# Two gated linear-recurrence blocks behind a transformer: key and query norms through a matrix of ones, the delta rule's preparation one level earlier

## What is computed

```
def _l2norm(x):
    return x * lax.rsqrt(jnp.sum(x * x, axis=-1, keepdims=True) + EPS)

def _gated_delta_rule(q, k, v, beta, g):        # chunks of 64 tokens
    gc = jnp.cumsum(g.reshape(b, h, n, c), axis=-1)
    decay = jnp.exp(jnp.where(incl, gc[..., :, None] - gc[..., None, :], -jnp.inf))
    kb = k * beta[..., None]
    a = jnp.where(strict, jnp.einsum('bhntd,bhnsd->bhnts', kb, k) * decay, 0.0)
    t_inv = lax.linalg.triangular_solve(a + eye, ...)      # (I + A)^-1
    qk = jnp.einsum('bhntd,bhnsd->bhnts', q, k) * decay
    ...

def _mixer(h, w_in, ...):
    p = h @ w_in
    (qkv, z, beta_r, a_r, hq, hf_fwd, hf_bwd, hi, hgate, gate_dn, gate_hg) = _split(p, IN_SIZES)
    qkv = jax.nn.silu(_dwconv(qkv, dn_conv))
    q = _l2norm(_to_heads(q, DN_HEADS)) * (DN_HEAD_DIM ** -0.5)
    k = _l2norm(_to_heads(k, DN_HEADS))
    ...
```

## Time and profile before

| | us |
|---|---|
| median of three runs | 2322.2 (2317.95 to 2328.46) |
| the profiled execution, its own time | 2322.91 |
| its span in the profile | 2320.8 |
| TensorE busy | 2208.2 (95% of the span) |
| VectorE, ScalarE, GpSimd busy | 1556.5, 1053.2, 183.9 |
| `square_sums` to `hg_o`, first mixer layer | 1372.06 to 1488.69 (starts) |

### The profile page before, as it was taken

The page is one execution under the profiler, slowest core; times in us unless marked ns, Lnnn a source line. Parts: engine busy times, 40 slices in busy tenths (PEclk is TensorE's granted clock), DMA queues, the critical chain, the costliest instruction groups (busy, mean ns, idle before and its releaser), DMA issues.

```text
span 2320.8 us, 39379 instructions
## 1 busy us (share of the span) xinstructions
PE 2208.2 (95%) x15834; PEld 2061.6 (89%) x15834; DVE 1556.5 (67%) x2334; ACT 1053.2 (45%) x1488; POOL 183.9 (8%) x157
## 2 busy tenths in 40 slices
PE   7999989999999999999998998999999998999997
PEld 7998869989999998798997998898998998898996
DVE  4557656755575575667557678867677678867676
ACT  4335465533353445554333555434344555434342
POOL 0000000131000000000000006300000006300000
PEclk9999989999999999999999999999999999999999
DMA  7454424475555554344553442214554432214553
GB/s 254 181 183 164 161 73 164 142 206 190 206 198 183 182 187 157 123 150 166 187 191 132 165 144 91 74 55 159 186 181 163 174 135 91 74 55 167 188 181 127
DMA packets 52667, 359.12 MB, mean 155 GB/s; under 512 B 6401, under 2 KB 6785, under 8 KB 11073
## 3 DMA queue, kind: packets, MB, share of 16 engines
q1 hardware_dynamic: 46928, 340.81, 41.4%
q0 software_dynamic: 4336, 13.37, 2.1%
q10 hardware_dynamic: 1280, 3.19, 0.4%
HBM read 356.29 MB, written 1.05 MB: 154 GB/s over the span
## 4 chain that ended last, share of the span: by engine, by line
PE 77%; DVE 12%; ACT 5%; DMA 4%; issue 2%; SPq 0%; DVEq 0%; POOLq 0%; ACTq 0%
PE tile L755 42%; PE acc L791 19%; PE tile L771 6%; DMA ring<-weights 4%; DVE ring_lo L1814 3%; PE tile L1082 3%; PE tile L1280 2%; ACT w_hi L1351 2%; PE tile L927 1%; PE tile L901 1%; PE tile L806 1%; DVE work L2304 1%; DVE work L2302 1%; DVE bn L2199 1%; PE tile L914 1%
## 5 line engine op out<-in xcount | busy, mean ns | idle before, releaser
L1814 DVE TENSOR_TENSOR ring_lo<-ring,w_hi 128x1024 fp32r<-128x1024 f32 x648 | 785.8, 1244 | 608.2 <-ACT w_hi L1351 605.8
L1351 ACT ACTIVATE w_hi<-ring 128x1024 fp32r<-128x1024 f32 x648 | 657.5, 1053 | 938.9 <-DMA ring<-weights 713.8
L755 PE MATMUL tile<-xT_hi,w_hi 128*128 128x256 f32 x3008 | 858.1, 285 | 16.8 <-DVE xT_lo L1805 13.9
L755 PE MATMUL tile<-xT_lo,w_hi 128*128 128x256 f32 x3008 | 853.0, 284 | 0.0
L755 PE MATMUL tile<-xT_hi,ring_lo 128*128 128x256 f32 x3008 | 852.9, 284 | 0.0
L755 PEld LDWEIGHTS tile<-xT_hi,w_hi 128*128 128x128 f32 x3008 | 579.2, 193 | 23.2 <-issue 12.3
L755 PEld LDWEIGHTS tile<-xT_lo,w_hi 128*128 128x128 f32 x3008 | 579.3, 193 | 2.2
L755 PEld LDWEIGHTS tile<-xT_hi,ring_lo 128*128 128x128 f32 x3008 | 579.0, 192 | 0.0
L791 PE MATMUL acc<-w_hi,hidden_hi 128*128 128x512 f32 x528 | 207.9, 394 | 5.5 <-DVE ring_lo L1814 5.5
L791 PE MATMUL acc<-w_hi,hidden_lo 128*128 128x512 f32 x528 | 207.2, 392 | 0.0
L791 PE MATMUL acc<-ring_lo,hidden_hi 128*128 128x512 f32 x528 | 206.6, 391 | 0.0
(11 more groups left out here) (272 smaller groups left out, 2740.7 us busy)
## 6 DMA issues: line engine op xcount, KB each, us to landing
ring<-weights SPq DMA_DIRECT2D x324, 1024.0 KB, 4.8
work<-ln_g_rows POOLq DMA_DIRECT2D x8, 512.0 KB, 6.1
work<-ln_b_rows POOLq DMA_DIRECT2D x8, 512.0 KB, 6.8
work<-rpb POOLq DMA_DIRECT2D x32, 96.0 KB, 14.3
x<-x_in SPq DMA_DIRECT2D x1, 1024.0 KB, 8.0
work<-mem_in ACTq DMA_DIRECT2D x1, 1024.0 KB, 6.6
out<-x POOLq DMA_DIRECT2D x1, 1024.0 KB, 4.4
work<-hmask_in ACTq DMA_DIRECT2D x1, 840.0 KB, 8.5
```

The costliest lines, as they stand in the source:

```text
L755: j = mm(ps[:, f * S:(f + 1) * S], w[a][:, k, :], x2[b][:, k, :], start=(k == 0 and i == 0), stop=(k == KT - 1 and i == 2))
L1351: A(high_of(u, h), half_of(ring, u, h), ACT.Copy).then_inc(sems["w_hi"], 1)
L1814: V.tensor_tensor(half_of(ring_lo, u, h), half_of(ring, u, h), high_of(u, h).bitcast(F32), ALU.subtract).then_inc(sems["w_lo"], 1)
```

## The change

- `square_sums` becomes four matmuls of 512 columns with the 128 x 128 matrix of ones as weights: each sum comes out spread over all partitions, in four tiles (`l2` has four instead of one).
- ScalarE computes from them, between its SiLUs of `hz` and `z`, the factor by logarithm and exponential: four `Ln` from PSUM into `l2s`, four `Exp` in place, with one table set named for both. The root, the reciprocal and the tiles `l2B` go. VectorE multiplies queries and keys by `l2s` out of SBUF between the low parts of the units that `z` feeds.
- `G` moves from level 3 to 2, `kv_T` from 4 to 3, `QK` from 5 to 4. `near_start` moves from behind `args` of level 3 to between the two halves of gate unit 2.
- The gate unit's halves are placed one by one: level 7 now gets the first half of gate unit 7, level 8 the second. The substitution's rows stand behind halves of gate units 3 to 7 and behind levels 4 to 8.
- GpSimd's list is reordered so that the decays are masked one `qmul` earlier.
- Two constants for the logarithm's bias are written by VectorE once, before the first mixer.

```diff
-PREP.update({0: (("gcB0", 2),), 1: (("gcB1", 2),), 2: (("l2B", 4),),
-             3: (("G", 2),), 4: (("kv_T", 4),), 5: (("QK", 2),)})
-GATE_AT = {k: k for k in range(7)}
-GATE_AT[8] = 7
+PREP.update({0: (("gcB0", 2),), 1: (("gcB1", 2),), 2: (("G", 2),), 3: (("kv_T", 4),), 4: (("QK", 2),)})
+GATE_AT = {k: ((k, 0), (k, 1)) for k in range(7)}
+GATE_AT[7] = ((7, 0),)
+GATE_AT[8] = ((7, 1),)
-NEAR_IN_GATE = {4: ((0, 7), (1, 7)), 5: ((0, 7), (1, 3), (1, 7)), 6: ((0, 7), (1, 3), (1, 7)), 7: ((0, 7),)}
+NEAR_AFTER_HALF = ((3, 0), (3, 1), (4, 0), (4, 1), (5, 0), (5, 1), (6, 0), (6, 1), (7, 0))
...
                 def square_sums():
-                    pe.wait_ge(sems["l2_sq"], 4 * l + 4)
-                    ps = open_tile(T[("l2", l)])
-                    for c in range(16):
-                        i = mm(ps[:, c:c + 1], l2s[:, c // 2, (c % 2) * P:(c % 2 + 1) * P], table("ones")[:, 0:1],
-                               start=True, stop=True)
-                    i.then_inc(sems["tile_ready"], 1)
+                    for j in range(4):
+                        pe.wait_ge(sems["l2_sq"], 4 * l + j + 1)
+                        ps = open_tile(T[("l2", l)] + j)
+                        mm(ps[:, :], table("ones"), pair(l2s, j), start=True, stop=True).then_inc(sems["tile_ready"], 1)
...
+                nc.scalar.preload_act_table_set("natural_log_exp_and_others")
+                for j in range(4):
+                    t = T[("l2", l)] + j
+                    act.wait_ge(*ready(t))
+                    A(pair(l2s, j), bank[t % NB][:, :], ACT.Ln, bias=l2_eps[:, 0:1] if j < 2 else l2_eps[:, 1:2],
+                      scale=float(P) if j < 2 else 1.0).then_inc(tile_taken[t % NB], 1)
+                for j in range(4):
+                    act.wait_ge(*taken(T[("l2", l)] + j))
+                    A(pair(l2s, j), pair(l2s, j), ACT.Exp, scale=-0.5).then_inc(sems["l2_inv"], 1)
...
-                for j in range(2):
-                    feed_one("z", j)
+                feed_one("z", 0)
+                for j in range(4):
+                    dve.wait_ge(sems["l2_inv"], 4 * l + j + 1)
+                    V.tensor_tensor(pair(qkvT, j), pair(qkvT, j), pair(l2s, j), ALU.mult).then_inc(sems["l2_done"], 1)
+                feed_one("z", 1)
...
+                    for g, half in GATE_AT[k]:
+                        if half == 0 and k < LEVELS:
+                            args(l, k + 2)
+                        if half == 1 and k == 2:
+                            near_start()
+                        if (g, half) in NEAR_AFTER_HALF:
                             near_step(next(rows))
+                        feed(U[("gate", l, g)], halves=(half,))
...
-                for k in range(1, 4):
+                for k in range(1, 3):
                     qmul(k)
-                    if k > 1:
-                        decays_of(2 * k - 4)
-                        decays_of(2 * k - 3)
-                qmul(4)
+                    decays_of(2 * k - 2)
+                    decays_of(2 * k - 1)
+                qmul(3)
```

More of the change, by code:

```diff
@@ L624, in build @@
         note = small[:, 13, :]
-        l2n, l2i, ngc = [small[:, i, :] for i in range(14, 17)]
+        l2_eps, ngc = small[:, 14, 0:2], small[:, 16, :]
         ba32 = small[:, 0:2, :].rearrange("p a b -> p (a b)")
@@ L743, in await_x, with features @@
                 pe.wait_ge(sems["x_lo"], 4 * plan.sets[name] + q + 1)
-            def features(u, t, x_set=None, more=0, x2=x2, between=None):
-                for f in range(2):
+            def features(u, t, x_set=None, more=0, x2=x2, halves=(0, 1)):
+                for f in halves:
                     w = open_half(u, f, KT, more)
-                    if f == 0:
-                        ps = open_tile(t, more)
+                    ps = open_tile(t, more) if f == 0 else bank[t % NB]
                     for k in range(KT):
@@ L1196, in mixer2 @@
                     prepare(k)
-                    if k in GATE_AT:
-                        g = GATE_AT[k]
-                        features(U[("gate", l, g)], T[("gate", l, g)],
-                                 between=lambda f, j: (f, j) in NEAR_IN_GATE.get(g, ()) and near_row(next(rows)))
+                    for g, half in GATE_AT[k]:
+                        features(U[("gate", l, g)], T[("gate", l, g)], halves=(half,))
+                        if (g, half) in NEAR_AFTER_HALF:
+                            near_row(next(rows))
                 for c in range(2):
@@ L1740, in mixer2 @@
                     prepare(k)
-                    if k in GATE_AT:
-                        feed(U[("gate", l, GATE_AT[k])])
-                        take(T[("gate", l, GATE_AT[k])], pair(gates, GATE_AT[k]))
+                    for g, half in GATE_AT[k]:
+                        split_half(U[("gate", l, g)] + 2, half)
+                        if half == 1:
+                            take(T[("gate", l, g)], pair(gates, g))
                 for g in range(4):
@@ L2419, in prepare @@
                     if k == 2:
-                        for j in range(4):
-                            t = T[("l2B", l)] + j
-                            dve.wait_ge(*ready(t))
-                            V.tensor_tensor(pair(qkvT, j), pair(qkvT, j), bank[t % NB][:, :], ALU.mult).then_inc(tile_taken[t % NB], 1)
-                        for j in range(4):
-                            dve.wait_ge(*taken(T[("l2B", l)] + j))
-                        dve.sem_inc(sems["l2_done"], 1)
-                    if k == 3:
                         for tt in range(TT):
@@ L2470, in mixer2 @@
                     prepare(k)
-                    at = NEAR_IN_GATE.get(GATE_AT.get(k), ())
-                    for f, j in at:
-                        if f == 0:
-                            near_step(next(rows))
-                    if k < LEVELS:
-                        args(l, k + 2)
-                    if k == 3:
-                        near_start()
-                    if k in GATE_AT:
-                        for f, j in at:
-                            if f == 1 and j < KT - 1:
-                                near_step(next(rows))
-                        feed(U[("gate", l, GATE_AT[k])], halves=(0,))
-                        for f, j in at:
-                            if f == 1 and j == KT - 1:
-                                near_step(next(rows))
+                    for g, half in GATE_AT[k]:
+                        if half == 0 and k < LEVELS:
+                            args(l, k + 2)
+                        if half == 1 and k == 2:
+                            near_start()
+                        if (g, half) in NEAR_AFTER_HALF:
+                            near_step(next(rows))
+                        feed(U[("gate", l, g)], halves=(half,))
                         if k == LEVELS + 1:
```

63 lines of the change are left out of this document (24 added, 39 removed).

## The result

The median of five executions of the changed kernel is 2310.66 us (2303.78 to 2314.39) against 2323.21 (2317.95 to 2328.46) before. The ratio is 0.9943, 95% interval 0.9922 to 0.9963: 12.6 us or 0.57% faster. Forecast were 2312.5 us and a range of 2305 to 2321. Repeated beside other kernels the changed one took 2311.23 us, ratio 0.9943 again (0.9923 to 0.9963).

What follows compares the result with a forecast made beforehand. TensorE, busy for 95% of the span, was taken as the bound, with its waits and lowered clock. Terms of -4.4 us (first layer), -6.2 (second) and 0.3 lost gave -10.3 us, so 2312.5 us, range 2305 to 2321.

Steps and rivals of the forecast that it cites:

- Norms and clock: From sums to level 0: full-array sums keep the clock up over `z`, saving 2.4 us (first layer), 4.2 (second).
- Spreading the norms: Dropping `l2B` saves 3.6 us a layer; its gather wait moves to gate unit 2 as 2.6 us, 0.4 lost.
- Start of the substitution: `near_start` a level sooner: 5.9 us of waiting moves to the third `kv_T` tile, clock falls as before; no gain.
- Last level: Half a gate unit between levels 7 and 8 covers `qmul(8)`; the wait goes, 2.7 us saved a layer.
- The rows: Substitution rows at new places wait 7.2 us for VectorE's steps; 2.9 us lost a layer, bounds 0 and 5.1.
- Behind the walk: At the third `W0` tile TensorE waits, as `x_first` stands behind the last low part; 1.0 us lost a layer.
- Rival 1: Clock stays up behind the `kv_T` wait: 2.2 us more saved a layer, 2308 us; chance 0.25.
- Rival 2: Clock still falls at the norms, taking back some 7.2 us: 2319.7 us; chance 0.22 together with Rival 3.
- Rival 3: The gather wait at gate unit 2 swallows the norms' saving, 6.4 us: 2319 us; chance 0.22 together with Rival 2.
- Rival 4: GpSimd's six operations between levels 5 and 8 each hit a substitution step: slower, 2337 us; chance 0.08.

Runs made afterwards that it cites:

- the best kernel: Changed kernel with the multiplies by beta moved to ScalarE and unread filler matmuls at `kv_T`, `W0` and in the recursion: 2302.54 us, ratio 0.9909.

## Why the forecast held, step by step

The 2312.5 us itself has a small slip in it: -10.3 us from the profiled execution is 2312.6, and an execution 0.7 us above the median puts the median at 2311.9. Of the chances, 0.37 went to a gain of more than 0.5%, and the 0.57% measured fell there, not into the 0.55 for less.

**Norms and clock: right.** -2.6 and -4.1 against -2.4 and -4.2. 1.6 us of the second layer's share hung on which profile of before it was read from. The added wait was 0.3 us, not 0.8. The load and the logarithm took what was forecast (load from 1365.25, next pass at 1366.55, so 1.30 and no drain), but the SiLU ahead of them began 1.2 us behind the sums' start instead of 1.7. Over all profiles with the new norms this wait is 0.3 to 0.7 us. That thin matmuls bring the clock down was argued in the prediction and is shown by the kernel that put them back.

**Spreading the norms: right, with a wait missed.** Gate unit 2 waits 2.26 us on the gather (forecast 2.6), but gate unit 1 waits 0.66 as well, which I had not: 0.7 us lost instead of 0.4. The second profile of before has a wait of 0.54 us at gate unit 1 in its first layer, so part of this is not the change's.

**Start of the substitution: right on the wait, the clock's part a little too dear.** The wait went to the third `kv_T` tile, 5.0 and 6.1 us against a forecast of 5.9, and the clock falls behind it as before. But only eight of the sixteen transposes stand behind it now; the other eight run at full clock ahead of it. Without the wait the sixteen take 2.7 us, where they took 3.5 to 3.6 in the first profile of before; in the second layer half of this 0.9 us goes again in the gate unit behind them, which takes more of the fall. The first layer's wait is shorter because TensorE arrived later: a half-clock stretch in gate unit 2 cost 1.5 us, 1.1 of which the wait gave back.

**Last level: right in the changed kernel, too small as a price.** The 2.7 us wait is gone. Undoing the split cost 4.2 us up to `hg_o`, since the wait is 3.4 us in the new order and a clock fall follows it.

**The rows: the term that was mis-sized.** Three waits of 1.10, 1.64 and 0.80 us, 3.5 in all against 2.1: 1.4 us lost, where I had 2.9. The prediction asked for 5 to 7 us on L2448, and this was wrong. Three of its five places were right, rows 5 and 8 and the hit of `qmul(8)` on row 12's step, each 0.4 to 0.6 us shorter than I had them; the 1.9 us for `qmul(7)` did not come. Row 8's step had ended 0.2 us before `qmul(7)` began (1453.75, 1453.93). So level 0 to `hg_o` gave 4.7 to 5.0 us instead of 3.0, the rows' 1.5 us being the larger part of the difference and the transposes a smaller one, and hg_o came 7.5 and 8.9 us sooner, beyond the 7 that I had named as the limit (in the repeated changed kernel's first layer, at 110.7, it is 5.9). The bound of 0 to 5.1 held it.

**Behind the walk: right.** 1.2 us of wait, 1.3 in all, against 1.0.

**What no term had: the late fall.** It took back 3.2 us of the first layer, so the sum came out at -10.6 where -10.3 was forecast: two misses, of -3.7 us over both layers' levels and +3.2 in the recursion, nearly cancel. That the forecast was close is in part their doing.

**The rivals.** Rival 1 (clock stays up behind the `kv_T` wait) did not occur in the four layers of the changed kernel's two profiles; it took fillers or another order to get there. Rival 2 (clock still falls at the norms) occurred in none of them either. Rival 3, that waits for the gather take the saving over, took 0.7 us in the changed kernel. With the norms changed alone it took 2.8 us in the first layer, the clock included, and nothing in the second; that this kernel measured only -2.7 us is mostly the late fall. Rival 4 stayed off, with three collisions that TensorE pays for. `qmul(5)` stretched row 3's step to 2.18 us, and `QK`'s products, the arguments and row 4's step follow it, for which row 5 waits 1.10 us. `row_gains` behind `qmul(6)` stretched arguments ahead of row 7's step to 3.42 us, and row 8 waits 1.64. `qmul(8)` hit row 12's step, and row 13 waits 0.80. Both engines in the changed kernel:

```profile
1434.36 2.39 POOL L2692 TENSOR_TENSOR work<-work 128x1024 f32<-128x1024 f32 x1 [6.13 <-ACT work L1634]
...
1434.66 2.18 DVE L2448 TENSOR_TENSOR work<-work 128x64 f32<-128x64 f32 x1
...
1446.88 2.43 POOL L2682 TENSOR_TENSOR work<-work,const 128x1024 f32<-128x1024 f32 x1
...
1446.98 3.42 DVE L2301 TENSOR_TENSOR work<-work 128x1024 f32<-128x1024 f32 x1
...
1464.29 2.39 POOL L2692 TENSOR_TENSOR work<-work 128x1024 f32<-128x1024 f32 x1 [7.14 <-ACT work L1634]
...
1464.74 2.17 DVE L2448 TENSOR_TENSOR work<-work 128x208 f32<-128x208 f32 x1
```

**What stays open.** Why the late fall is absent from all four layers of the kernel before. The kernel with the norms alone has the same instructions in the recursion and had it in both. A filler ahead of it and one in the `W0` wait keep it away (none in six layers of three kernels), but what decides whether it comes without them was not found. Four layers are also few. Nor were `G` and `kv_T` a level earlier, the start of the substitution and the rows' places undone one by one: their terms are read from the waits in the profiles.

## What to carry to other kernels

- Cut both spans at the same instructions before explaining a difference. Here 8.6 of 19 us lay ahead of the first changed instruction.
- A wait's price is its length plus what the clock does behind it. Useless wide matmuls in a wait that can't be removed kept the clock up behind it: with all four waits filled no stretch of either layer was at half clock.
- When moving work on a waiting engine moves the wait and not the sum, add up busy times of the engines that share an access, and take work off them. Two reorderings gained nothing, nor did a third on top of the best kernel; one product moved to an engine with time to spare shortened the waits.

## What the runs showed of the chip

**The same instructions, another clock.** In the changed kernel's two layers the stretches ahead of the late fall read alike in busy time and count, and one fell and the other did not. The Trainium skill (TensorE: Matmul & The Clock Gate, Part 1: The HAM clock gate) says that the number of matmuls at the low clock at a kernel's start varies from run to run of one kernel. The two profiles of the changed kernel agree in the middle of it (the first layer's late fall is 8 us long in one and 11 in the other), and the rows show that it also varies between two like places of one execution. The changed kernel's five executions order themselves by it: 2303.8 us at a mean clock of 0.988, 2309.6 at 0.986, 2310.7 at 0.983, 2312.7 and 2314.4 at 0.982.

**Busy is not full.** Thin matmuls at 4.00 of 4.00 us busy ended at a clock of 0.50. The falls in gate unit 2, at `kv_T` and in the recursion followed waits of 2.3, 5 to 6 and only 0.8 us, the last among matmuls of 64 and 128 columns.

**GpSimd and VectorE take turns.** The Trainium skill (GPSIMD Engine Reference, Specifications) has the two share their SBUF interfaces when VectorE reads two SBUF inputs. The rows agree: arguments of 1.2 us, both inputs in SBUF, took 3.42 beside GpSimd, and 7.8 us less of GpSimd took 4.2 us off VectorE's own busy time.
